# Four split-weight buffers given start addresses of their own in a three-pass float32 matmul kernel on one Trainium2 core

## The chip, the cores and the metric

The kernel runs on one core of a Trainium2 chip. The metric is the device time of one execution in microseconds (us). The profile calls the engines PE (TensorE, matmuls), PEld (TensorE's weight loads, which overlap its matmuls), DVE (VectorE), ACT (ScalarE), POOL (GpSimd) and SP (SyncE, which issues the loads). In a matmul one operand is stationary (the 128x128 block that a weight load brings into the array) and the other is moving (here mostly 128 partitions by 512 columns).

## The reference, cut to what matters

The reference is a stack of layers on 512 tokens of width 1024 in float32: a token mixer of four groups of heads, a short-convolution mixer, a latent attention, and three gated feed-forward layers of inner width 2816. Most of its arithmetic is products of activations with weight matrices:

```
x = x + mixed.astype(x.dtype) @ w_out[l]
x = x + conv_glu_ffn(rms_norm(x, norm2_g[l]), w_up[l], ffn_conv_w[l], ffn_conv_b[l], w_down[l])
...
u = h @ w_in
...
return (jax.nn.silu(g) * u) @ w2
```

## The kernel before, in words

**Weights.** The weight matrices are cut into 297 units of up to 1024 columns per partition (UNIT: eight 128x128 blocks, 4096 bytes in each partition). SP loads unit u into slot u % 4 of `raw` (L326, L338). ACT copies it into `whi` in the rounded type float32r (L352, slot u % 2), and DVE subtracts that from `raw` and writes the rest to `wlo` (L360, slot u % 2). So there are four split-weight buffers: two of `whi` and two of `wlo`.

**Products.** PE waits for the split of its unit and then does, for each 128-row block k, three matmuls (`passes`, L365 to L367): `whi` block times high part of the activation, `whi` block times low part, `wlo` block times high part. Each has its own weight load. The activations stand as `xhi`/`xlo`, `h_hi`/`h_lo`, `c_hi`/`c_lo`, `chi`/`clo` or `lhi`/`llo`, tiles of 512 columns. At the last matmul of a unit the semaphore `unit_used` goes up, which lets ACT split the unit after the next (L351). In one part of the latent attention `lhi`/`llo` are stationary and `whi`/`wlo` blocks are moving.

**Order.** The order of the work on every engine is written out by hand and synchronised by semaphores; nothing of it depends on an address. The matmuls that are not weight products (transposes, attention, scans) work on plain float32 tiles: `cst` (constant matrices), `mx`, `kn`, `qn`, `vtok` and others. Of them `pe_head_norm` (L876) has a block of `cst` stationary, and the attention logits (L1900, L1901) and outputs (L1610) have activations stationary.

**Addresses.** SBUF buffers are laid one after the other in the order of their declaration, each start rounded up to 32 bytes. Ahead of `whi` stand `xT`, `xhi`, `xlo` and `raw`, each 16384 bytes per partition, and the first of them starts 128 bytes past a multiple of 512. So do `xhi`, `xlo`, `raw`, both slots of `whi` and both of `wlo`. The buffers from `cst` up to the activations of the later layers take 27136 bytes (53 times 512), so that `h_hi`, `h_lo`, `c_hi`, `c_lo`, `lhi`, `llo`, `chi` and `clo` start at 128 past a multiple of 512 as well; `sq` starts at 416 past one. Each tile of 512 columns is 2048 bytes and each 128-column block 512 bytes. The blocks of `cst` used as stationary operands stand 516 bytes or 516 plus a multiple of 512 bytes into `cst`, that is at 132 past a multiple of 512.

Of the kernel before, what the change touches and what calls it, by code (L numbers as in the profile page):

```python
# [15 lines left out]
F32R = mybir.dt.float32r  # L16
I32 = mybir.dt.int32
ALU = mybir.AluOpType
ACT = mybir.ActivationFunctionType
AX = mybir.AxisListType  # L20

P = 128
# [13 lines left out]
UNIT = KT * P  # L36
RAW = 4
PARTS = 2
# [194 lines left out]
def build(nc, A, cst_d, out_d, known):  # L233
    ctx = ExitStack()
    with ctx:
        def sb(name, shape, dt=F32, c=ctx):
            return c.enter_context(nc.sbuf_tensor(name, shape, dt))

        def sem(name):
            return ctx.enter_context(nc.semaphore(name))  # L240
# [3 lines left out]
        xhi = sb("xhi", [P, KT, T], F32R)  # L244
        xlo = sb("xlo", [P, KT, T], F32R)
        raw = sb("raw", [P, RAW, UNIT])
        whi = sb("whi", [P, PARTS, UNIT], F32R)
        wlo = sb("wlo", [P, PARTS, UNIT], F32R)
        cst = sb("cst", [P, NCONST])
        pcol = sb("pcol", [P, NPCOL])  # L250
        gbias = sb("gbias", [P, 4])
# [29 lines left out]
        hi_split, lo_split, unit_used = sem("hi_split"), sem("lo_split"), sem("unit_used")  # L281
# [8 lines left out]
        v, a, g, t_ = nc.vector, nc.scalar, nc.gpsimd, nc.tensor  # L290

        def f32(ap):
            return ap.bitcast(F32)
# [13 lines left out]

        def unit_view(buf, u):
            _, kt, n, _ = UNITS[u]
            return buf[:, u % (RAW if buf is raw else PARTS), 0:kt * n].rearrange("p (k c) -> p k c", c=n)  # L310

        def is_past(u, i, per):
            return u + (per * i if isinstance(i, int) else 0) >= len(UNITS)

        def in_loop(value, i, per):
            return value if i is None else value + per * i

        def load_unit(sp, u):
            name, kt, n, pieces = UNITS[u]
            if u >= RAW:  # L320
                sp.wait_ge(lo_split, u - RAW + 1)
            at = 0
            for r0, c0, m in pieces:
                dst = unit_view(raw, u)[:, :, at:at + m]
                src = A[name][r0:r0 + kt * P, c0:c0 + m].rearrange("(k p) c -> p k c", p=P)
                sp.dma_start(dst, src).then_inc(unit_loaded[u % RAW], 16)  # L326
                at += m

        def load_loop(sp, stage, n_units, per, col):

            with sp.Fori(0, n_units // per) as i:
                for j in range(per):
                    u = FIRST[stage] + j
                    name, kt, n, pieces = UNITS[u]
                    r0 = pieces[0][0]
                    sp.wait_ge(lo_split, u - RAW + 1 + per * i)
                    src = A[name][r0:r0 + kt * P, bass.ds(col(i, j), n)].rearrange("(k p) c -> p k c", p=P)
                    sp.dma_start(unit_view(raw, u), src).then_inc(unit_loaded[u % RAW], 16)  # L338

        def elements(u, i, per):  # L340
            units = [UNITS[u]] + ([UNITS[u + per]] if i is not None and u + per < len(UNITS) else [])
            return max(kt * n for _, kt, n, _ in units)

        def split_hi(act, u, i=None, per=0):

            if is_past(u, i, per):
                return
            n = elements(u, i, per)
            act.wait_ge(unit_loaded[u % RAW], in_loop(LOADED[u], i, 16 * per // RAW))
            if u >= PARTS:  # L350
                act.wait_ge(unit_used, in_loop(u - PARTS + 1, i, per))  # L351
            a.activation(whi[:, u % PARTS, 0:n], raw[:, u % RAW, 0:n], ACT.Copy).then_inc(hi_split, 1)  # L352

        def split_lo(dve, u, i=None, per=0, e=v):

            if is_past(u, i, per):
                return
            n = elements(u, i, per)
            dve.wait_ge(hi_split, in_loop(u + 1, i, per))
            e.tensor_tensor(wlo[:, u % PARTS, 0:n], raw[:, u % RAW, 0:n], f32(whi[:, u % PARTS, 0:n]),  # L360
                            ALU.subtract).then_inc(lo_split, 1)

        def passes(out, wh, wl, xh, xl, first, last):
# [5 lines left out]
        def product(pe, u, tile, i=None, per=0, x=(xhi, xlo), k0=0, start=True, stop=True, ready=None, cols=0,  # L369
                    full=None, order=None, ks=None):  # L370


            kt = UNITS[u][1]
            pe.wait_ge(lo_split, in_loop(u + 1, i, per))
            for n, k in list(enumerate(order or range(kt)))[slice(*(ks or (0, kt)))]:
                if ready is not None:
                    ready(pe, k0 + k)
                wh, wl = (unit_view(b, u)[:, k, cols:cols + P] for b in (whi, wlo))
                last = passes(acc(tile), wh, wl, x[0][:, k0 + k, :], x[1][:, k0 + k, :],
                              start and n == 0, stop and n == kt - 1)  # L380
            if ks is None or ks[1] == kt:
                last.then_inc(*(step("pe", full) if full else (unit_used, 1)))
# [98 lines left out]
        def act_residual(act, stage, thirds, gain, following=None):  # L481
            per, np_, tiles = round_of(thirds)
            r0, n0 = NORM0[stage], TILE0[stage]

            def square(i, m):
                act.wait_ge(acc_free, n0 + m + 3 + tiles * i)
                act.wait_ge(summed, r0 + m + 1 + tiles * i)
                a.activation(sq[:, m % 2, :], tile_of(xT, m + tiles * i), ACT.Square).then_inc(squared, 1)  # L488

            def body(i, begun):  # L490
                for j in range(per):
                    m = j // np_
                    if begun and j == per - 1:
                        used = FIRST[stage] + KT // tiles * per
                        act_gain_all(act, begun, used, range(KT // 2))
                        square(i, m)
                        act_gain_all(act, begun, used, range(KT // 2, KT))
                    split_hi(act, FIRST[stage] + j + 2, i, per)
                    if j % np_ == np_ - 1 and not (begun and j == per - 1):
                        square(i, m)  # L500
                        if gain:
                            act.wait_ge(squared, r0 + m + 1 + tiles * i)
                            act_gained(act, gain, m + tiles * i)
            rounds(act, stage, KT // tiles, body, following)
# [53 lines left out]
        def act_up(act, stage, conv, h_hi, zS, yg, yu):  # L558
            u0, p0, n0 = FIRST[stage], PAIR0[stage], TILE0[stage]
            a.preload_act_table_set("silu_and_others")  # L560
            with act.Fori(0, FT // 2) as i:
                for j in range(4):
                    pair, is_up = j // 2, j % 2
                    m = pair + 2 * i
                    split_hi(act, u0 + j + 2, i, 4)
                    if conv:
                        mt = m + FT * is_up
                        act.wait_ge(prod_done, p0 + pair + 1 + 2 * i)
                        act.wait_ge(acc_free, n0 + j + 3 + 4 * i)
                        a.activation((yu if is_up else yg)[:, pair, :], zS[:, is_up, :], ACT.Identity,  # L570
                                     scale=ffn_w(2, mt), bias=ffn_b(mt)).then_inc(tap_done, 1)
                        if is_up:
                            act.wait_ge(conv_done, j + 2 + 4 * i)
                            a.activation(yg[:, pair, :], yg[:, pair, :], ACT.Silu).then_inc(gated, 1)
                    elif not is_up:
                        act.wait_ge(acc_free, n0 + j + 3 + 4 * i)
                        a.activation(yg[:, pair, :], zS[:, 0, :], ACT.Silu).then_inc(gated, 1)
                    if is_up:
                        act.wait_ge(prod_done, p0 + pair + 3 + 2 * i)
                        a.activation(tile_of(h_hi, m), xg[:, pair, :], ACT.Copy).then_inc(prod_hi, 1)  # L580
# [1833 lines left out]
def _program(nc, arrays, known):  # L2414

    aps = {n: nc.dram_tensor(f"in_{n}", a.shape, mybir.dt.from_np(a.dtype), kind="ExternalInput").ap()
           for n, a in arrays.items()}
    out = nc.dram_tensor("out_0", _OUT, F32, kind="ExternalOutput").ap()
    cst = aps.pop("constants")
    flat = {n: (x[0] if len(x.shape) == 3 and n in _WEIGHTS else x) for n, x in aps.items()}  # L2420
    return build(nc, flat, cst, out, known)
# [34 lines left out]
```

## Time and profile before

| | |
|---|---|
| time, 3 runs | 1982.45, 1982.6, 1985.07 us; median 1982.6 |
| profiled execution | 1982.77 us, span from first to last instruction 1981.0 us |
| mean granted TensorE clock | 0.985 of full speed |
| PE busy | 1905.2 us, 96% of the span |
| PEld busy | 1543.1 us, 78% |
| DVE, ACT, POOL busy | 997.3 us, 749.4 us, 228.9 us |

The profile is of one execution. A busy time counts from an instruction's start to its end, and matmuls overlap each other: one that takes 0.39 us can start 0.23 us after the one before. So the distance from start to start tells the pace of PE, not the duration of one.

### The profile page before, as it was taken

How to read it: one execution, taken by the hardware profiler on the slowest of the kernel's cores; microseconds unless marked ns; L12 is line 12 of the kernel's file. 1: busy time of each engine (PE TensorE's matmuls, PEld its weight loads, DVE VectorE, ACT ScalarE, POOL GpSimd, SP SyncE). 2: the span in 40 equal slices, each digit the busy share in tenths (PEclk: the TensorE clock that was granted, in tenths of full speed). 3: DMA queues.
4: the chain of work that ended last, by engine and by line, in shares of the span. 5: the costliest groups of instructions: out<-in, count | busy, mean ns of one | idle time of the engine just before them, and what ended most of it. 6: DMA issues, size and time to landing. Idle time of an engine off the chain costs nothing.

```text
span 1981.0 us, 25408 instructions
## 1 busy us (share of the span) xinstructions
PE 1905.2 (96%) x8897; PEld 1543.1 (78%) x8897; DVE 997.3 (50%) x1467; ACT 749.4 (38%) x1081; POOL 228.9 (12%) x196
## 2 busy tenths in 40 slices
PE   7989978889999999999999999999999999999998
PEld 6778856567788888888878888888776778888887
DVE  5463478754677774344454444433557443434322
ACT  5542543443544443232233323222455443222322
POOL 0051000012111111100021111110000111111100
PEclk9999989899999999999999999999999999999999
DMA  6310210011333333333333333333321123333332
GB/s 188 86 32 1 54 33 22 22 64 54 95 95 95 95 93 97 97 96 98 101 89 96 95 95 95 92 97 98 91 80 43 33 85 96 97 99 99 89 97 72
DMA packets 309219, 161.23 MB, mean 81 GB/s; under 512 B 12688, under 2 KB 306832, under 8 KB 309024
## 3 DMA queue, kind: packets, MB, share of 16 engines
q1 hardware_dynamic: 308080, 157.64, 27.6%
q0 software_dynamic: 640, 2.17, 0.3%
q8 instruction: 43, 0.70, 0.1%
q10 hardware_dynamic: 432, 0.52, 0.1%
q14 instruction: 24, 0.20, 0.0%
HBM read 158.21 MB, written 2.10 MB: 81 GB/s over the span
## 4 chain that ended last, share of the span: by engine, by line
PE 90%; DVE 5%; ACT 2%; issue 2%; DMA 1%; SPq 0%; POOL 0%; DVEq 0%; ACTq 0%; POOLq 0%
PE ps L365 26%; PE ps L367 26%; PE ps L366 26%; PE ps L1404 1%; PE ps L1019 1%; PE ps L1610 1%; PE ps L1419 1%; PE ps L1031 1%; PE ps L1900 1%; PE ps L1901 1%; PE ps L892 1%; PE ps L1395 1%; PE ps L1601 1%; DMA mx<-in_x 0%; PE ps L1239 0%
## 5 line engine op out<-in xcount | busy, mean ns | idle before, releaser
L365 PE MATMUL ps<-xhi,whi 128*128 128x512 f32 x1656 | 661.5, 399 | 10.1 <-DVE xlo L437 6.7
L366 PE MATMUL ps<-xlo,whi 128*128 128x512 f32 x1656 | 646.2, 390 | 0.0
L367 PE MATMUL ps<-xhi,wlo 128*128 128x512 f32 x1656 | 646.1, 390 | 0.0
L352 ACT ACTIVATE whi<-raw 128x1024 fp32r<-128x1024 f32 (+2 forms) x297 | 308.9, 1040 | 716.1 <-PE ps L367 713.5
L360 DVE TENSOR_TENSOR wlo<-raw,whi 128x1024 fp32r<-128x1024 f32 (+2 forms) x297 | 365.8, 1232 | 281.3 <-ACT whi L352 281.2
L365 PEld LDWEIGHTS ps<-xhi,whi 128*128 128x128 f32 x1656 | 312.0, 188 | 82.3 <-issue 5.4
L367 PEld LDWEIGHTS ps<-xhi,wlo 128*128 128x128 f32 x1656 | 311.8, 188 | 66.0
L366 PEld LDWEIGHTS ps<-xlo,whi 128*128 128x128 f32 x1656 | 312.1, 188 | 65.4 <-issue 3.7
L594 DVE TENSOR_TENSOR zS<-ps,rs 128x512 f32<-128x512 f32 x132 | 91.3, 692 | 293.7 <-PE ps L367 284.6
L367 PE MATMUL ps<-h_hi,wlo 128*128 128x512 f32 x528 | 205.4, 389 | 0.0
L365 PE MATMUL ps<-h_hi,whi 128*128 128x512 f32 x528 | 205.4, 389 | 0.0
L366 PE MATMUL ps<-h_lo,whi 128*128 128x512 f32 x528 | 205.4, 389 | 0.0
L619 POOL TENSOR_TENSOR h_lo<-xg,h_hi 128x512 f32 x66 | 84.9, 1286 | 646.3 <-ACT h_hi L580 646.3
L535 POOL TENSOR_TENSOR ssq<-ssq,sq 128x512 f32<-128x512 f32 x48 | 76.1, 1585 | 562.3 <-ACT sq L488 562.3
L366 PEld LDWEIGHTS ps<-h_lo,whi 128*128 128x128 f32 x528 | 99.1, 188 | 20.7
L367 PEld LDWEIGHTS ps<-h_hi,wlo 128*128 128x128 f32 x528 | 99.1, 188 | 20.7
L365 PEld LDWEIGHTS ps<-h_hi,whi 128*128 128x128 f32 x528 | 99.1, 188 | 20.2
L516 DVE TENSOR_TENSOR xT<-ps,xT 128x512 f32<-128x512 f32 (+1 forms) x48 | 33.2, 692 | 129.3 <-PE ps L367 129.3
L580 ACT ACTIVATE h_hi<-xg 128x512 f32 x66 | 41.7, 632 | 144.7 <-DVE xg L610 144.7
L1404 PE MATMUL ps<-mx,cst 128*128 128x512 f32 (+15 forms) x128 | 45.7, 463 | 27.1 <-DVE mx L1480 18.6
L1404 PEld LDWEIGHTS ps<-mx,cst 128*128 128x128 f32 x128 | 24.5, 212 | 41.5 <-DVE mx L1480 25.2
L437 DVE SCALAR_TENSOR_TENSOR xlo<-xT,pcol,xhi 128x512 fp32r<-128x512 f32 (+1 forms) x48 | 46.7, 1003 | 13.4 <-ACT xhi L431 13.2
(320 smaller groups left out, 1784.1 us busy)
## 6 DMA issues: line engine op xcount, KB each, us to landing
raw<-in_conv_ffn_w SPq DMA_DIRECT2D x52, 512.0 KB, 3.8
raw<-in_mla_ffn_w SPq DMA_DIRECT2D x52, 512.0 KB, 3.8
raw<-in_w_up SPq DMA_DIRECT2D x44, 512.0 KB, 3.7
raw<-in_w_in SPq DMA_DIRECT2D x28, 512.0 KB, 3.8
raw<-in_conv_w_in SPq DMA_DIRECT2D x24, 512.0 KB, 3.7
raw<-in_w_down SPq DMA_DIRECT2D x16, 448.0 KB, 3.6
raw<-in_conv_ffn_w SPq DMA_DIRECT2D x16, 448.0 KB, 3.6
raw<-in_mla_ffn_w SPq DMA_DIRECT2D x16, 448.0 KB, 3.6
```

Source lines behind the costliest of these rows:

```text
L352: a.activation(whi[:, u % PARTS, 0:n], raw[:, u % RAW, 0:n], ACT.Copy).then_inc(hi_split, 1)
L360: e.tensor_tensor(wlo[:, u % PARTS, 0:n], raw[:, u % RAW, 0:n], f32(whi[:, u % PARTS, 0:n]), ALU.subtract).then_inc(lo_split, 1)
L365: t_.matmul(out, wh, xh, start=first, stop=False)
L366: t_.matmul(out, wh, xl, start=False, stop=False)
L367: return t_.matmul(out, wl, xh, start=False, stop=last)
L437: v.scalar_tensor_tensor(tile_of(xlo, k), tile_of(xT, k), gain_of(name, k), f32(tile_of(xhi, k)), ALU.mult, ALU.subtract).then_inc(x_lo, 1)
L516: v.tensor_tensor(x, acc(m), x, ALU.add).then_inc(acc_free, 1)
L535: g.tensor_tensor(ssq[:, :], ssq[:, :], sq[:, m, :], ALU.add).then_inc(summed, 1)
L580: a.activation(tile_of(h_hi, m), xg[:, pair, :], ACT.Copy).then_inc(prod_hi, 1)
L594: v.tensor_tensor(z, acc(j), rs[:, :], ALU.mult).then_inc(acc_free, 1)
L619: g.tensor_tensor(tile_of(h_lo, m + 2 * i), xg[:, m, :], f32(tile_of(h_hi, m + 2 * i)), ALU.subtract).then_inc(prod_lo, 1)
L1404: t_.matmul(out[:, 0:n], C(red), PROD[j % 3][:, 0:n], start=True, stop=True).then_inc(*step("pe", f"{nm} intra{j} {vi} full"))
```

## The change

`whi` and `wlo` become four tensors, each of one unit (4096 bytes per partition), with unused gaps of 64, 64, 128 and 256 bytes behind them. Nothing but addresses is altered: the same instructions in the same order read and write buffers at 128 (`whi_a`), 192 (`whi_b`), 256 (`wlo_a`) and 384 (`wlo_b`) bytes past a multiple of 512. The gaps come to 512 bytes, so that every buffer behind them moves up by 512 bytes.

```
-        whi = sb("whi", [P, PARTS, UNIT], F32R)
-        wlo = sb("wlo", [P, PARTS, UNIT], F32R)
+        whi_a = sb("whi_a", [P, UNIT], F32R)
+        gap_a = sb("gap_a", [P, 16])
+        whi_b = sb("whi_b", [P, UNIT], F32R)
+        gap_b = sb("gap_b", [P, 16])
+        wlo_a = sb("wlo_a", [P, UNIT], F32R)
+        gap_c = sb("gap_c", [P, 32])
+        wlo_b = sb("wlo_b", [P, UNIT], F32R)
+        gap_d = sb("gap_d", [P, 64])
+        whi, wlo = (whi_a, whi_b), (wlo_a, wlo_b)
...
-            return buf[:, u % (RAW if buf is raw else PARTS), 0:kt * n].rearrange("p (k c) -> p k c", c=n)
+            slot = raw[:, u % RAW, 0:kt * n] if buf is raw else buf[u % PARTS][:, 0:kt * n]
+            return slot.rearrange("p (k c) -> p k c", c=n)
...
-            a.activation(whi[:, u % PARTS, 0:n], raw[:, u % RAW, 0:n], ACT.Copy).then_inc(hi_split, 1)
+            a.activation(whi[u % PARTS][:, 0:n], raw[:, u % RAW, 0:n], ACT.Copy).then_inc(hi_split, 1)
...
-            e.tensor_tensor(wlo[:, u % PARTS, 0:n], raw[:, u % RAW, 0:n], f32(whi[:, u % PARTS, 0:n]),
+            e.tensor_tensor(wlo[u % PARTS][:, 0:n], raw[:, u % RAW, 0:n], f32(whi[u % PARTS][:, 0:n]),
```

## Rows read from the trace of the kernel before

**Rows 1.** The page: busy time of each engine, and the chain that ended last.

```profile
span 1981.0 us, 25408 instructions
...
PE 1905.2 (96%) x8897; PEld 1543.1 (78%) x8897; DVE 997.3 (50%) x1467; ACT 749.4 (38%) x1081; POOL 228.9 (12%) x196
...
PE 90%; DVE 5%; ACT 2%; issue 2%; DMA 1%; SPq 0%; POOL 0%; DVEq 0%; ACTq 0%; POOLq 0%
PE ps L365 26%; PE ps L367 26%; PE ps L366 26%; PE ps L1404 1%; PE ps L1019 1%; PE ps L1610 1%; PE ps L1419 1%; PE ps L1031 1%; PE ps L1900 1%; PE ps L1901 1%; PE ps L892 1%; PE ps L1395 1%; PE ps L1601 1%; DMA mx<-in_x 0%; PE ps L1239 0%
```

**Rows 2.** Three stretches: length, busy time and count by engine, clock, DMA.

```profile
620.00:820.00 200.00, 200.00 (x884) 165.60 (x883) 115.95 (x130) 74.91 (x96) 23.14 (x18) 1.00 0.33 95
1120.00:1420.00 300.00, 300.00 (x1324) 248.12 (x1323) 115.13 (x122) 90.23 (x107) 34.22 (x27) 1.00 0.34 97
1720.00:1900.00 180.00, 180.00 (x796) 149.10 (x795) 66.71 (x74) 53.40 (x65) 21.91 (x17) 1.00 0.33 96
```

**Rows 3.** Timeline of PE in a feed-forward layer: start us, duration us, instruction.

```profile
1250.00 0.39 PE L365 MATMUL ps<-xhi,whi 128*128 128x512 f32 x1
...
1251.59 0.39 PE L366 MATMUL ps<-xlo,whi 128*128 128x512 f32 x1
```

**Rows 4.** Timeline of the weight loads in the same stretch.

```profile
1250.00 0.19 PEld L366 LDWEIGHTS ps<-xlo,whi 128*128 128x128 f32 x1
1250.23 0.19 PEld L367 LDWEIGHTS ps<-xhi,wlo 128*128 128x128 f32 x1
```

**Rows 5.** Groups by line and shape, PE: busy us, mean ns | idle before.

```profile
L365 PE MATMUL ps<-xhi,whi 128*128 128x512 f32 x1656 | 661.5, 399 | 10.1 <-DVE xlo L437 6.7 <-DVE wlo L360 3.4
...
L365 PE MATMUL ps<-h_hi,whi 128*128 128x512 f32 x528 | 205.4, 389 | 0.0
...
L365 PE MATMUL ps<-c_hi,whi 128*128 128x512 f32 x64 | 25.6, 399 | 2.2 <-POOL c_lo L619 2.2
...
L365 PE MATMUL ps<-chi,whi 128*128 128x512 f32 x36 | 14.9, 415 | 0.3 <-ACT qp L1949 0.3
...
L365 PE MATMUL ps<-lhi,whi 128*128 128x512 f32 x16 | 7.1, 444 | 0.0
...
L365 PE MATMUL ps<-whi,lhi 128*128 128x512 f32 x16 | 6.4, 402 | 1.4 <-ACT vtok L1936 1.4
```

**Rows 6.** Timeline of PE in the attention logits, plain float32.

```profile
1500.20 1.02 PE L1900 MATMUL ps<-kn,qn 128*128 128x512 f32 x2
1501.06 1.02 PE L1901 MATMUL ps<-kpz,qp 128*128 128x512 f32 x2
```

**Rows 7.** Timeline of PE where a block of cst is stationary.

```profile
94.39 1.88 PE L876 MATMUL ps<-sq,cst 128*128 128x512 f32 x4
```

**Rows 8.** Groups by line and shape, weight loads (PEld): busy us, mean ns.

```profile
L365 PEld LDWEIGHTS ps<-xhi,whi 128*128 128x128 f32 x1656 | 312.0, 188 | 82.3 <-issue 5.4 <-DVE xT L516 4.2 <-DVE xlo L437 2.9
...
L1019 PEld LDWEIGHTS ps<-mx 128*128 128x128 f32 x224 | 27.5, 205 | 0.9 <-POOL mx L981 0.9
...
L1901 PEld LDWEIGHTS ps<-kpz,qp 128*128 128x128 f32 x64 | 11.6, 190 | 6.4 <-issue 3.8
...
L1900 PEld LDWEIGHTS ps<-kn,qn 128*128 128x128 f32 x64 | 9.9, 190 | 0.7 <-ACT mla_P L1625 0.3
...
L876 PEld LDWEIGHTS ps<-sq,cst 128*128 128x128 f32 x32 | 6.2, 195 | 4.5 <-issue 3.1 <-ACT sq L858 0.5 <-DVE mx L883 0.2
...
L1826 PEld LDWEIGHTS ps<-qn,cst 128*128 128x128 f32 x10 | 1.9, 189 | 1.6 <-issue 1.4
```

**Rows 9.** Line views of both splits, 1250 to 1258: min/median/max ns, first to last start.

```profile
L352 ACT ACTIVATE whi<-raw x2: 1062/1062/1062, 1251.6 to 1257.0; 128x1024 fp32r<-128x1024 f32 x2
...
L360 DVE TENSOR_TENSOR wlo<-raw,whi x1: 1225/1225/1225, 1252.7 to 1252.7; 128x1024 fp32r<-128x1024 f32 x1
```

**Rows 10.** Tile wlo, whole span: all its splits, and its readiness as a cause of waiting.

```profile
L360 DVE TENSOR_TENSOR wlo<-raw,whi x297: 952/1226/1710, 14.4 to 1960.0; 128x1024 fp32r<-128x1024 f32 x127, 128x896 fp32r<-128x896 f32 x19, 128x768 fp32r<-128x768 f32 x3
```

## The prediction

> **What bounds the kernel now.** I read the page first: PE is busy for 96% of the span, and the chain that ended last lies on PE for 90% of it, 78% on the three lines of `passes` alone [rows 1]. A kernel in that state is as long as its matmuls are apart, so the next view is a table of stretches in the long feed-forward layers. There PE is busy for all of 200, 300 and 180 us, at a granted clock of 1.00, which is the 2.4 GHz level; it starts 884, 1324 and 796 matmuls in them [rows 2]. Divided, that is 226.2, 226.6 and 226.1 ns per matmul, a little low since a matmul cut by the edge of a stretch counts. The timeline gives the pace itself: from 1250.00 to 1251.59 us there are seven starts after the first, so 227 ns from each to the next [rows 3]. The three passes come at one pace, through layers in which DVE is busy for 58% of the time and for 37% of it [rows 2], so what sets the pace is in PE and its operands and not in what the other engines happen to do.
>
> The number to keep is what 227 ns is made of. 512 columns at 2.4 GHz are 213.3 ns; the pace is 13.3 ns more, or 544 clock periods where the tile has 512 columns. The next weight load starts with the running matmul (1250.00 and 1250.00 us) and lasts 188 ns, so it is over some 38 ns before the next start [rows 3, 4, 8]. Whether those 13.3 ns are a fixed price of changing weights, or two reads of SBUF in each other's way, is the whole question, because addresses are all that is changed.
>
> **The change part by part.** No instruction is added, removed or moved, and no wait. Four things get other addresses.
>
> *Weight loads from `whi_b`, `wlo_a` and `wlo_b`.* The lines of L365 add up to 1656 + 528 + 64 + 36 + 16 = 2300 blocks with weights stationary [rows 5], so 6900 loads for three passes. Two thirds come from `whi`, and units alternate between its slots: 2300 each from `whi_a` and `whi_b`, 1150 each from `wlo_a` and `wlo_b`. `whi_a` stays at 128, so 4600 loads read from a new phase. The trace has no float32r matmul at another phase: the moving tiles too start at 128 past a multiple of 512, all of them. The nearest rows are the plain float32 matmuls. L1900 and L1901 have both operands at multiples of 512 from 128, and L1901 starts 0.86 us after the first of two L1900, 430 ns each [rows 6]. L876 has a `cst` block at 132 stationary and `sq` at 416 moving; its four last 1.88 us in all, and with 0.59 for the last one (1.02 - 0.43 by the logits) the starts are 430 ns apart [rows 6, 7]. The loads themselves take 190 ns from `qn` and `qp` and 189 from `cst` at L1826; the 195 of L876 and 205 of L1019 are means over groups with some longer ones [rows 8]. So two pairs of phases, the stationary ones not even 16-byte aligned to each other, give one pace and nearly one load. That is the value I take: 4600 times 0 = 0. It doesn't prove it for float32r, where the moving tile goes by at twice the pace and has half as much room for a second reader. The bound below is that all 13.3 ns go: 4600 x 13.3 = 61 us gained. The bound above is the longest of these load rows, if the 38 ns between a load's end and the next start stay as they are: 205 + 38 = 243 ns, 16 more than now, 4600 x 16 = 74 us lost.
>
> The Trainium skill speaks on this (SBUF — State Buffer, "Who interferes with whom"): PE has one read port for the moving operand and an independent one for weight loads, and never waits on another engine. By it the loads' phase costs and gains nothing, and the sum is the same 0; but it leaves the 13.3 ns unexplained, and no row here shows the ports.
>
> *The v part of the latent attention*, with `whi`/`wlo` blocks moving and `lhi`/`llo` stationary: 16 blocks of three passes [rows 5], 48 matmuls. At the same bounds, 48 x 13.3 = 0.6 us either way, two thirds of them moved; 0 taken.
>
> *The splits.* ACT writes `whi` in 1062 ns and DVE reads it and writes `wlo` in 1225 ns. What hides them is the unit in the array: ACT starts at 1251.6 us, DVE ends at 1252.7 + 1.2 = 1253.9, and the release of the next slot, with which PE goes on to this unit, is at 1257.0, 3.1 us later [rows 9]. A split would have to grow by more than its own length to be seen. Where there is less cover, in the mixers and at the layers' starts, PE waited for `wlo` for 3.4 us of the whole span [rows 5]; splits slower by a tenth would make that less than 1 us more. The spread that is already there, 952 to 1710 ns [rows 10], includes smaller units and meetings with POOL, and the latter don't depend on 64 bytes. 0 taken.
>
> *Everything behind*, from `cst` on, moves by 512 bytes and keeps its phase, so the loads, stores and 1949 other matmuls (8897 less 6900 and 48) see no other alignment. 0.
>
> The sum: 0 + 0 + 0 + 0. The profiled execution took 1982.77 us, 0.2 us from the median 1982.6 of the runs, so I predict the median, 1982.6 us. Within 0.2% of it, 1978.6 to 1986.6, is about what a measurement of this kernel can't tell from no change; the three runs alone spread over 2.6 us.
>
> **Rival 1: faster, the reads were in each other's way.** For it: the excess is 32 periods per 512 columns and keeps to the same value in every layer, which reads in step with each other would give, and a weight block and its moving tile stand at one phase in every float32r pair. Plain float32 matmuls, at half the pace, have almost no excess: 430 ns for what would be 426.7 [rows 6]. Against it: the load ends well before the matmul does, so a shift of 64 bytes shifts the meeting in time more than it undoes it; and a fixed price would look the same. If the excess fell to the 3.3 ns of the float32 rows in the moved loads, 4600 x 10 = 46 us go and the time is 1937 us; with all of it gone, 1922. If only the `wlo` loads (2300) gain, 1960. The sign to look for is a pace that differs between buffers, L365 to L367 in units of odd number against even ones.
>
> The Trainium skill has a rule of this kind (TensorE: Matmul & The Clock Gate, "Back-to-back issue gap"): at full clock one matmul follows another by N/2.4 + 2.5 ns, 216 for 512 columns. The trace doesn't agree, at 227 ns; if the alignment were why, the rule would make it 4600 x 11 = 51 us less, an estimate of 1932 us.
>
> **Rival 2: slower, one phase was what kept them apart.** The mechanism: with moving tile and weight block at one phase, the two reads go through SBUF in step; at 64, 128 and 256 bytes' distance some meet, and a load or a matmul grows. It costs where the array is never idle, so each nanosecond counts: 0.2% of 1982.6 is 4.0 us, over 4600 loads 0.86 ns each, and that is the point from which it decides. At the upper bound, 16 ns, the time is 1982.6 + 74 = 2056 us; should just the 2300 `wlo` loads take the mean load of L876, 7 ns more, it is 1982.6 + 16 = 1999 us. Against it stand the 430 ns at both pairs of phases [rows 6, 7].
>
> **Rival 3: a small drift,** 4 to 10 us either way, from a few waits and clock drops that fall otherwise, in the mixers, where the chain leaves PE for 10% of the span [rows 1]. Nothing is changed there in kind, and the three runs say 2.6 us.
>
> **How the numbers follow.** No change 0.82; rival 1, 0.08; rival 2, 0.07; rival 3, 0.03, shared between the signs. That gives faster by over 0.2% 0.09, within 0.2% 0.83, slower 0.08. The range is that of the likeliest case, which alone holds 8 in 10: 1978.6 below and, as one of the runs stood 2.5 us above the median, a little over 1986.6 above, so 1978 to 1988. The unknown costs' bounds, 1922 and 2056, belong to the rivals and are left outside; they hold less than 2 in 10 together.
>
> **What would show it.** In the profile of the changed kernel: 25408 instructions [rows 1]; the three stretches with 884, 1324 and 796 matmuls within one or two; loads of 188 ns from all four buffers; both splits at about 1062 and 1225 ns; PE at 96%. The prediction is wrong if the starts of L365 to L367 are apart by anything but 227 ns in any buffer: 217 says rival 1, over 228 rival 2. If they stand at 227 and the time is still off, the step on the splits or the other buffers has failed, and waits for `wlo` at L365 would show above 3.4 us.

## The result, and the profile after

The changed kernel takes 2015.92 us (median of 4 runs, 2012.94 to 2017.64) against 1982.96 us (4 runs, 1982.45 to 1985.07): a ratio of 1.0161, 95% interval 1.0148 to 1.0173, or 33 us more. It is slower, and the time lies outside the range of the prediction.

The page of the changed kernel, its head and its chain, beside [rows 1]:

```profile
span 2014.3 us, 25408 instructions
...
PE 1938.3 (96%) x8897; PEld 1548.3 (77%) x8897; DVE 994.3 (49%) x1467; ACT 751.4 (37%) x1081; POOL 229.5 (11%) x196
...
PE 90%; DVE 5%; ACT 2%; issue 2%; SPq 0%; DMA 0%; POOL 0%; DVEq 0%; ACTq 0%; POOLq 0%
```

The instructions are the same, and so is the chain, to a point in the shares. PE's busy time is up by 33.1 us, which is the whole loss; PEld's is up by 5.2 us, 0.6 ns per load, and DVE, ACT and POOL are within 3 us. Nothing waits for anything new. Three stretches of the feed-forward layers show it, beside [rows 2] (length, busy time and count of PE, PEld, DVE, ACT, POOL, then the granted clock):

```profile
620.00:820.00 200.00, 200.00 (x866) 162.77 (x865) 116.71 (x135) 76.20 (x96) 21.76 (x18) 1.00 0.32 94
1140.00:1440.00 300.00, 300.00 (x1297) 243.83 (x1296) 112.58 (x120) 88.35 (x107) 34.31 (x27) 1.00 0.33 94
1750.00:1930.00 180.00, 180.00 (x780) 146.49 (x779) 65.54 (x72) 51.99 (x64) 21.97 (x17) 1.00 0.33 95
```

At the same clock, 2.4 GHz, PE starts 866 matmuls in the first stretch where it started 884: 200/866 = 230.9 ns against 226.2. The rows by line tell the buffers apart. These are the down projections, whose moving tiles are `h_hi` and `h_lo` (busy us, mean ns of one | idle before); a unit in slot a is read from `whi_a` and `wlo_a`, one in slot b from `whi_b` and `wlo_b`:

```profile
L374 PE MATMUL ps<-h_lo,whi_b 128*128 128x512 f32 x264 | 104.8, 397 | 0.0
L375 PE MATMUL ps<-h_hi,wlo_a 128*128 128x512 f32 x264 | 104.6, 396 | 0.0
L374 PE MATMUL ps<-h_lo,whi_a 128*128 128x512 f32 x264 | 104.5, 396 | 0.0
L375 PE MATMUL ps<-h_hi,wlo_b 128*128 128x512 f32 x264 | 104.0, 394 | 0.0
L373 PE MATMUL ps<-h_hi,whi_a 128*128 128x512 f32 x264 | 103.2, 391 | 0.0
L373 PE MATMUL ps<-h_hi,whi_b 128*128 128x512 f32 x264 | 102.7, 389 | 0.0
```

Before, each of the three passes was 389 ns, the first in [rows 5] and the other two in the same view:

```profile
L366 PE MATMUL ps<-h_lo,whi 128*128 128x512 f32 x528 | 205.4, 389 | 0.0
L367 PE MATMUL ps<-h_hi,wlo 128*128 128x512 f32 x528 | 205.4, 389 | 0.0
```

There a matmul was 389 ns and its successor started 227 ns after it, so about 162 ns of a duration overlap the next one and the rest is the pace; what a duration has above 389 is taken as time lost. The six rows come to 623.8 us for 1584 matmuls, 393.8 ns each, 4.8 ns more than before; times the 6948 float32r matmuls that is 33 us. (In what follows "excess" is this number for a slot: its three h rows, divided by 792, less 389.0. The ends of matmuls are modelled in the profile, so behind it, in brackets, stands the same from the start times in the trace: the mean from one start to the next, less the 226.7 ns of the kernel before. The two differ by up to 1.1 ns.) Slot a, in which `whi_a` has not moved in phase, has 5.3 ns (4.9) and slot b 4.3 (4.6). The 4968 matmuls with x tiles went the same way, from a mean of 393.3 ns to 398.5.

The loads have hardly changed, beside the 188 ns of [rows 8], and neither have the splits, in the view by line and shape over all engines:

```profile
L368 DVE TENSOR_TENSOR wlo_a<-raw,whi_a 128x1024 fp32r<-128x1024 f32 x127 | 156.3, 1231 | 97.0 <-ACT whi_a L360 97.0
...
L360 ACT ACTIVATE whi_a<-raw 128x1024 fp32r<-128x1024 f32 x127 | 134.6, 1059 | 399.8 <-PE ps L375 398.6 <-DMA raw<-in_w_in 1.2
...
L375 PEld LDWEIGHTS ps<-h_hi,wlo_b 128*128 128x128 f32 x264 | 49.6, 188 | 10.2
L374 PEld LDWEIGHTS ps<-h_lo,whi_a 128*128 128x128 f32 x264 | 49.6, 188 | 11.3
...
L1908 PE MATMUL ps<-kn,qn 128*128 128x512 f32 x16 | 8.2, 593 | 0.0
```

The last row is the attention logit matmul in plain float32, and it has not moved either. Before:

```profile
L1900 PE MATMUL ps<-kn,qn 128*128 128x512 f32 x16 | 8.2, 593 | 0.0
```

### The profile page after: what moved, and what is told of

Read it like the earlier page. It is cut to its first block, busy times and chain, and to the rows that moved or that the text cites. A ratio compares the mean times of both kernels' runs of the same rounds, so it can differ in the third digit from the quotient of the medians.

```text
span 2014.3 us, 25408 instructions
## 1 busy us (share of the span) xinstructions
PE 1938.3 (96%) x8897; PEld 1548.3 (77%) x8897; DVE 994.3 (49%) x1467; ACT 751.4 (37%) x1081; POOL 229.5 (11%) x196
## 4 chain that ended last, share of the span: by engine, by line
PE 90%; DVE 5%; ACT 2%; issue 2%; SPq 0%; DMA 0%; POOL 0%; DVEq 0%; ACTq 0%; POOLq 0%
PE ps L374 26%; PE ps L375 26%; PE ps L373 26%; PE ps L1412 1%; PE ps L1027 1%; PE ps L1618 1%; PE ps L1427 1%; PE ps L1039 1%; PE ps L1908 1%; PE ps L1909 1%; PE ps L900 1%; PE ps L1609 1%; PE ps L1403 1%; SPq L334 0%; PE ps L1711 0%
## 5 line engine op out<-in xcount | busy, mean ns | idle before, releaser
L373 PE MATMUL ps<-xhi,whi_b 128*128 128x512 f32 x824 | 330.5, 401 | 7.8 <-DVE xlo L445 4.6
L373 PE MATMUL ps<-xhi,whi_a 128*128 128x512 f32 x832 | 333.8, 401 | 2.0 <-DVE xlo L445 2.0
L375 PE MATMUL ps<-xhi,wlo_a 128*128 128x512 f32 x832 | 330.6, 397 | 0.0
L374 PE MATMUL ps<-xlo,whi_a 128*128 128x512 f32 x832 | 330.6, 397 | 0.0
L374 PE MATMUL ps<-xlo,whi_b 128*128 128x512 f32 x824 | 328.2, 398 | 0.0
L375 PE MATMUL ps<-xhi,wlo_b 128*128 128x512 f32 x824 | 326.0, 396 | 0.0
L368 DVE TENSOR_TENSOR wlo_a<-raw,whi_a 128x1024 fp32r<-128x1024 f32 (+2 forms) x149 | 180.0, 1208 | 149.1 <-ACT whi_a L360 149.1
L368 DVE TENSOR_TENSOR wlo_b<-raw,whi_b 128x1024 fp32r<-128x1024 f32 (+2 forms) x148 | 182.9, 1236 | 139.8 <-ACT whi_b L360 139.7
L373 PEld LDWEIGHTS ps<-xhi,whi_b 128*128 128x128 f32 x824 | 155.9, 189 | 51.9 <-DVE xT L524 4.2
L373 PEld LDWEIGHTS ps<-xhi,whi_a 128*128 128x128 f32 x832 | 159.5, 192 | 40.0 <-DVE kraw L2026 2.1
L374 PEld LDWEIGHTS ps<-xlo,whi_a 128*128 128x128 f32 x832 | 157.4, 189 | 35.6 <-issue 1.4
L375 PEld LDWEIGHTS ps<-xhi,wlo_a 128*128 128x128 f32 x832 | 157.2, 189 | 34.5
L375 PEld LDWEIGHTS ps<-xhi,wlo_b 128*128 128x128 f32 x824 | 155.7, 189 | 32.6
L375 PE MATMUL ps<-h_hi,wlo_a 128*128 128x512 f32 x264 | 104.6, 396 | 0.0
```

Source lines behind the costliest of these rows:

```text
L368: e.tensor_tensor(wlo[u % PARTS][:, 0:n], raw[:, u % RAW, 0:n], f32(whi[u % PARTS][:, 0:n]), ALU.subtract).then_inc(lo_split, 1)
L373: t_.matmul(out, wh, xh, start=first, stop=False)
L374: t_.matmul(out, wh, xl, start=False, stop=False)
L375: return t_.matmul(out, wl, xh, start=False, stop=last)
```

## The experiments

**Theories.** M: the pace depends on how far, in bytes, the weight block starts from the moving tile (below: the distance, 0 before the change, and 0, 64, 128 and 256 for `whi_a`, `whi_b`, `wlo_a`, `wlo_b` after it). S: it depends on the step in phase from one weight block to the next. A: some starts are bad in themselves. Each kernel below computes the same as the kernel before; only the lines that declare the buffers differ from the changed kernel, whose own four gaps are taken out in all of them. The rows shown of each are those by line and shape: busy us, mean ns of one | idle before; the three lines of `passes` lie between L370 and L375 there, always in the order `whi` with the high part, `whi` with the low part, `wlo`. While a matmul runs, the block of the next one is loaded, so an interval from start to start has one block in use and another on its way. "whi, wlo" of a slot means both of its buffers, and each kernel but e4 ends its gaps so that everything behind keeps its phase.

### e1: all four at distance 64

```
+        gap0 = sb("gap0", [P, 16])
         whi_a = sb("whi_a", [P, UNIT], F32R)
         whi_b = sb("whi_b", [P, UNIT], F32R)
         wlo_a = sb("wlo_a", [P, UNIT], F32R)
         wlo_b = sb("wlo_b", [P, UNIT], F32R)
+        gap1 = sb("gap1", [P, 112])
```

> All four buffers at 192 past a multiple of 512, the moving tiles still at 128. Theory M (the pace depends on how far the weight block stands from the moving tile): the distance is 64 in every load, so the pace leaves 227 ns, to 229 to 236, and the time is 1998 to 2030 us. Theory S (it depends on the step in phase from one weight block to the next): every step is 0 as before the change, the pace is 227 ns and the time 1983 us. Theory A (192, 256 or 384 are bad starts in themselves): 192 is one of them, slower as by M.

Measured: 2027.07 us, ratio 1.0218 (1.0189 to 1.0248). Slower than the change itself, with no step anywhere, so S falls as the whole cause. One row of slot a and one of slot b:

```profile
L371 PE MATMUL ps<-h_hi,whi_b 128*128 128x512 f32 x264 | 104.3, 395 | 0.0
...
L373 PE MATMUL ps<-h_hi,wlo_a 128*128 128x512 f32 x264 | 104.3, 395 | 0.0
```

All six are at 395: an excess of 6.1 ns (6.7), and 6948 x 6.1 = 42 us, of the 43 measured.

### e2: slot a at 0, slot b at 64

```
         whi_a = sb("whi_a", [P, UNIT], F32R)
         wlo_a = sb("wlo_a", [P, UNIT], F32R)
+        gap0 = sb("gap0", [P, 16])
         whi_b = sb("whi_b", [P, UNIT], F32R)
         wlo_b = sb("wlo_b", [P, UNIT], F32R)
+        gap1 = sb("gap1", [P, 112])
```

> Slots a (whi and wlo) at 128, slots b at 192. Within a unit all loads have one phase; only units differ. M and A: units in slots a keep 227 ns, units in slots b go to 229 to 236, time 1983 plus half of some 32, about 1990 to 2005 us. S: only the one load per unit that changes slot steps, 297 loads of at most 9 ns, so 1983 to 1986 us, both slots at 227 ns inside a unit.

Measured: 2009.78 us, ratio 1.0131 (1.0102 to 1.0161), some 5 us above the range that M gave: half of e1's 43 us would be 2006, and slot a was not quite free.

```profile
L371 PE MATMUL ps<-h_hi,whi_b 128*128 128x512 f32 x264 | 104.5, 396 | 0.0
L373 PE MATMUL ps<-h_hi,wlo_b 128*128 128x512 f32 x264 | 104.4, 396 | 0.0
L372 PE MATMUL ps<-h_lo,whi_b 128*128 128x512 f32 x264 | 104.4, 395 | 0.0
L372 PE MATMUL ps<-h_lo,whi_a 128*128 128x512 f32 x264 | 103.0, 390 | 0.0
L373 PE MATMUL ps<-h_hi,wlo_a 128*128 128x512 f32 x264 | 102.9, 390 | 0.0
L371 PE MATMUL ps<-h_hi,whi_a 128*128 128x512 f32 x264 | 102.7, 389 | 0.0
```

The slots go their own ways, unit by unit, in one run: 6.6 ns (6.7) in slot b, 0.6 (0.8) in slot a. So one run can measure two distances, to about 1 ns. The writes by ACT and DVE are not what is met. They go into the slot that PE is not reading, and in e1 the start times give 233.3 ns from start to start both in the intervals in which a split is running and in those in which none is.

### e3: whi at 0, wlo at 128

```
         whi_a = sb("whi_a", [P, UNIT], F32R)
         whi_b = sb("whi_b", [P, UNIT], F32R)
+        gap0 = sb("gap0", [P, 32])
         wlo_a = sb("wlo_a", [P, UNIT], F32R)
         wlo_b = sb("wlo_b", [P, UNIT], F32R)
+        gap1 = sb("gap1", [P, 96])
```

> Both whi at 128, both wlo at 256. S: two of three loads step by 128 or minus 128; they go to some 233 ns as in slot a of the changed kernel, the third stays at 227 to 229; 1982.6 + 6900 x 4.8 ns = about 2014 us. M and A: only the wlo loads are away from 128, one load in three is slower, by up to 9 ns: 2300 x 9 = 20 us, about 1990 to 2004 us, and the two intervals in which whi is loaded stay at 227.

Measured: 2010.68 us, ratio 1.0136 (1.0106 to 1.0165): above M's range and nearer to the number of S.

```profile
L373 PE MATMUL ps<-h_hi,wlo_a 128*128 128x512 f32 x264 | 104.8, 397 | 0.0
...
L372 PE MATMUL ps<-h_lo,whi_a 128*128 128x512 f32 x264 | 104.5, 396 | 0.0
...
L371 PE MATMUL ps<-h_hi,whi_a 128*128 128x512 f32 x264 | 102.7, 389 | 0.0
```

During L372 the next block, from `wlo`, is loaded: 7 ns longer, as M has it. During L373 a `whi` block at distance 0 is loaded, and that is 8 ns longer too, which M in its simple form did not give and S did. S as the whole cause fell with e1; what is left of it is that an interval's cost is not only that of the load in it.

### e4: all operands moved by 64, distances kept

```
+        front = sb("front", [P, 16])
         xT = sb("xT", [P, KT, T])
```

> 64 bytes ahead of the first buffer, so that all operands, moving and stationary, stand at 192 and keep their distances. M and S: 227 ns and 1983 us. A: every load is from a bad start, the pace is above 229 ns and the time above 1998 us.

Measured: 1983.73 us (8 runs), ratio 1.0001 (0.9990 to 1.0012). All h rows are back at 389 ns, as this one is:

```profile
L370 PE MATMUL ps<-h_hi,whi_a 128*128 128x512 f32 x264 | 102.7, 389 | 0.0
```

A falls for 192, which is as good a start as 128 if the moving tile is there too. It is also the control for taking the tensors apart, which costs nothing.

### f1 to f4, g2, g4, h2: other distances, two per run

These test three theories, named in the texts below: R, that the cost repeats at a shorter step of the distance than 512 bytes; L, that every distance but 0 costs alike; G, that some distance is better than 0. All runs have the shape of e2; slot a and slot b stand at the two distances in the name. Distances of 4, 16, 208 and 240 are not multiples of 32 and are made by a slice of a larger buffer. As examples:

```
+        gap0 = sb("gap0", [P, 32])                                  # f2
         whi_a = sb("whi_a", [P, UNIT], F32R)
         wlo_a = sb("wlo_a", [P, UNIT], F32R)
+        gap1 = sb("gap1", [P, 32])
...
-        whi_b = sb("whi_b", [P, UNIT], F32R)                        # g4
+        whi_b = sb("whi_b", [P, UNIT + 8], F32R)[:, 1:1 + UNIT]
```

> whi and wlo of slot a 32 bytes from the moving tile's phase, of slot b 96 bytes. Theory L (only distance 0 is good, any other costs about what 64 did, 6.6 ns a matmul): both slots at some 233 ns, time about 2027 us. Theory R (SBUF repeats at a shorter step than 512, so that some distances are as good as 0): 32 and 96 are not whole multiples of 64, so they go to 233 ns too unless the step is 32. Theory G (some distance is better than 0, down to 216 ns): one of the two slots below 227 ns.

> Slot a at distance 128, slot b at distance 256. L: both at 233 ns, about 2027 us. R: with a step of 128 both are back at 227 ns and the time at 1984 us; with a step of 256 only slot b, about 2005 us. G: a slot below 227 ns.

> Slot a at distance 384 (minus 128), slot b at 448 (minus 64). L: both at 233 ns, about 2027 us. R: as the same steps say, slot a back at 227 ns with a step of 128, else 233; slot b 233. G: if the sign of the distance matters, one of these is below 227 ns where 64 and 128 are above.

> Slot a at distance 16, slot b at distance 192. L: both at 233 ns, about 2027 us. If the cost grows with the distance, slot a stays near 227 ns and slot b at 233, about 2005 us. G: one below 227 ns.

> Slot a at distance 224, slot b at 240, that is 32 and 16 short of 256. Theory R with a cost that depends on the distance on the far side: 192 and 448 took 229 ns, so 224 and 240 take 227 to 230 ns and the time is 1984 to 2005 us. Theory L (any distance that isn't a multiple of 256 costs about 6 ns): both at 233 ns, about 2027 us. Theory G: one of them below 227 ns and the time below 1980 us.

> Slot a at distance 320, slot b at distance 4. R: slot a as at 64, some 233 ns. Slot b: if a 16-byte piece of SBUF is the unit in which reads meet, 4 bytes is partly in the same piece and takes 227 to 231 ns; if it is only a matter of the phase in time, 4 bytes are one column or 0.4 ns and it keeps 227. Time 1983.5 + 3450 x 6.6 ns = about 2006 us with slot b at 227, and up to 2018 us with it at 231.

> Slot a at distance 160, slot b at 208. From the distances so far (128 to 232.6 ns, 192 to 229.1, 224 to 233.2, 240 to 227.4) both lie between 227 and 234 ns and the time between 1990 and 2027 us. Theory G, some distance is better than 0: a slot below 226.6 ns.

Measured (ratio with its 95% interval; excess of a slot from its three h rows, in brackets from the start times):

| run | time us | ratio | slot a: distance, excess | slot b: distance, excess |
|---|---|---|---|---|
| f1 | 2028.48 | 1.0225 (1.0195 to 1.0255) | 32, 6.6 ns (6.7) | 96, 7.2 ns (7.3) |
| f2 | 2004.91 | 1.0106 (1.0077 to 1.0136) | 128, 5.6 ns (5.7) | 256, 0.5 ns (0.5) |
| f3 | 2010.17 | 1.0133 (1.0103 to 1.0162) | 384, 5.6 ns (5.9) | 448, 2.7 ns (2.5) |
| f4 | 2006.84 | 1.0116 (1.0087 to 1.0145) | 16, 2.0 ns (2.1) | 192, 2.5 ns (2.4) |
| g2 | 2010.30 | 1.0131 (1.0111 to 1.0152) | 224, 6.1 ns (6.8) | 240, 1.8 ns (1.9) |
| g4 | 2021.86 | 1.0190 (1.0169 to 1.0210) | 320, 5.4 ns (6.5) | 4, 4.9 ns (5.7) |
| h2 | 2023.35 | 1.0199 (1.0169 to 1.0229) | 160, 6.3 ns (7.0) | 208, 4.7 ns (5.2) |

Rows by line and shape of f2, where slot a (128) stands at 395 ns and slot b (256) is back at 389:

```profile
L372 PE MATMUL ps<-h_hi,whi_a 128*128 128x512 f32 x264 | 104.3, 395 | 0.0
...
L372 PE MATMUL ps<-h_hi,whi_b 128*128 128x512 f32 x264 | 102.7, 389 | 0.0
```

And of slot b of g4, where 4 bytes cost 5 ns:

```profile
L372 PE MATMUL ps<-h_lo,whi_b 128*128 128x512 f32 x264 | 104.0, 394 | 0.0
```

Distances that differ by 256 agree, by the start times: 0 and 256 (0.8, 0.5), 128 and 384 (5.7, 5.9), 192 and 448 (2.4, 2.5), 64 and 320 (6.7, 6.5). So theory R holds with a repeat of 256 bytes where both buffers of a slot share one distance, and L, all distances alike, falls: 192 and 240 cost about a third of 64 or 96. G falls as far as it was looked for: at fifteen distances other than 0 no slot's mean is below 389 ns, or below 226.7 from start to start. Not all came out as expected: g2 took 2010 us against 2005 at most and g4 2022 against 2018; 448 cost 2.5 ns where 6 were expected, the cost of 64; and f4 met its 2005 us with 2 ns in each slot and not 6 in one.

One distance does not have one cost. In f4 slot a has 2.0 ns with the h tiles, while with the x tiles its three rows are at 405, 395 and 394 against a mean of 393 before, 4.5 ns. By the start times, slot a of f4 has two paces, unit by unit. In all three down projections its first four units with h tiles are at 233.2 to 233.4 ns and the eight after them at 226.6 to 226.7, the pace of distance 0. After the first of the three it stays there through the x units that follow, up to 1004 us, where the x units before it, read from the same buffers, were at 233.3 to 233.4; at 1059 us, after some 50 us of other work, it is back at 233.3. One unit at each pace, from 766.7 and from 797.3 us:

```profile
L371 PE MATMUL ps<-h_hi,whi_a 128*128 128x512 f32 x8 | 3.2, 394 | 0.0
L371 PE MATMUL ps<-h_hi,whi_a 128*128 128x512 f32 x8 | 3.1, 389 | 0.0
```

So the 2.0 ns of 16 bytes is 12 units with the full cost and 24 with none. The same addresses can give either.

### g1: the weights left alone, the moving tiles moved

```
+        front = sb("front", [P, 48])
         xT = sb("xT", [P, KT, T])
...
+        gap0 = sb("gap0", [P, 80])
         whi_a = sb("whi_a", [P, UNIT], F32R)
...
+        gap1 = sb("gap1", [P, 16], c=mla)
         qn = sb("qn", [P, NH2, T], c=mla)
+        gap2 = sb("gap2", [P, 112], c=mla)
```

> All weight buffers back at 128; xT, xhi, xlo and raw at 320 instead, h_hi and h_lo at 128 as before. If the distance between the two operands is what counts, with a repeat of 256 bytes (theory R), the x passes are at distance 320, which is 64 past a multiple of 256, and take 233 ns, the h passes 227 ns: 4968 x 6.6 ns = 33 us, about 2016 us. If something about the weight buffers themselves counts, everything is at 227 ns and 1984 us. Besides, qn (stationary) stands 64 bytes from kn (moving) in the attention logits, plain float32: if the slower stream hides the meeting, L1900 keeps its 430 ns from start to start; if not, it goes up by 6 ns or more.

`front` pushes `xT`, `xhi`, `xlo` and `raw` to 320, and `gap0` puts the weights back to 128.

Measured: 2014.26 us, ratio 1.0151 (1.0131 to 1.0172).

```profile
L372 PE MATMUL ps<-xlo,whi_a 128*128 128x512 f32 x832 | 329.9, 396 | 0.0
L373 PE MATMUL ps<-xhi,wlo_a 128*128 128x512 f32 x832 | 329.7, 396 | 0.0
...
L371 PE MATMUL ps<-h_hi,whi_b 128*128 128x512 f32 x264 | 102.7, 389 | 0.0
L373 PE MATMUL ps<-h_hi,wlo_b 128*128 128x512 f32 x264 | 102.7, 389 | 0.0
...
L1908 PE MATMUL ps<-kn,qn 128*128 128x512 f32 x16 | 8.2, 593 | 0.0
```

This is the run that settles what counts. From the same weight buffers, the x passes lose 6 ns and the h passes nothing, according to where the other operand stands. And the logits, whose operands are now 64 bytes apart, stay at 593 ns: plain float32 does not show the effect.

### g3: the change in whole steps of 256 bytes

```
-        gap_a = sb("gap_a", [P, 16])
+        gap0 = sb("gap0", [P, 64])
```

and so behind each of the four: `whi_a` and `wlo_a` at 128, `whi_b` and `wlo_b` at 384.

> The change made again with whole steps of 256 bytes: whi_a and wlo_a at 128, whi_b and wlo_b at 384, a gap of 256 bytes behind each. R: all at 227 ns, 1984 us, the same as before. If different starts of the buffers cost something in themselves, above 1990 us.

Measured: 1984.14 us (10 runs) against 1984.16 us (13 runs), ratio 1.0003 (0.9994 to 1.0013).

```profile
L375 PE MATMUL ps<-h_hi,wlo_a 128*128 128x512 f32 x264 | 102.7, 389 | 0.0
L373 PE MATMUL ps<-h_hi,whi_b 128*128 128x512 f32 x264 | 102.7, 389 | 0.0
```

Four buffers apart, two phases, and no loss.

### h1: whi_b alone at 64

```
         wlo_b = sb("wlo_b", [P, UNIT], F32R)
+        gap0 = sb("gap0", [P, 16])
         whi_b = sb("whi_b", [P, UNIT], F32R)
+        gap1 = sb("gap1", [P, 112])
```

> Only whi_b is moved, to 192; the other three buffers at 128. If 256 is as good as 0, slot b behaves as in the changed kernel: intervals of some 226, 236 and 232 ns, 231.4 in the mean, slot a at 227: 1983.5 + 3450 x 4.7 ns = about 2000 us. If wlo_b at 384 had a share in the changed kernel, slot b is faster than 231.4 ns. If each load had a price of its own by its distance, the intervals in which whi_b is loaded would take 233 ns and the one in which wlo_b is loaded 227; if the cost is carried over from one matmul to the next, the one with the unmoved wlo_b is not 227.

Measured: 2008.89 us, ratio 1.0126 (1.0097 to 1.0156); 2000 was expected.

```profile
L371 PE MATMUL ps<-h_hi,whi_b 128*128 128x512 f32 x264 | 105.1, 398 | 0.0
L373 PE MATMUL ps<-h_hi,wlo_b 128*128 128x512 f32 x264 | 104.8, 397 | 0.0
L372 PE MATMUL ps<-h_lo,whi_b 128*128 128x512 f32 x264 | 103.5, 392 | 0.0
```

A miss. Slot b has an excess of 6.7 ns here (and slot a, unmoved, 1.0) and 4.3 in the changed kernel, where `wlo_b` stands 256 further. So the times of single loads cannot be added up, and 256 and 0 did not come to the same here: in this run the two intervals with a `whi_b` load are 9 and 8 ns longer and the one with `wlo_b` 3, in the changed kernel it is 0 and 5 for the first two and 8 for the last. In both runs part of the cost falls in an interval whose own load is at distance 0 or 256. Since f4 shows two paces at the same addresses, it is not shown that the 256 bytes make the difference: it may be the way into the pattern.

The start times show how long a cost is carried. They were averaged over the 12 stretches of exactly 24 h matmuls from one slot (in ns from start to start; the other slot was read just before each stretch; the last interval, in which the other slot's block is loaded, is left out):

| run, slot | first intervals | then |
|---|---|---|
| e2, slot a (0; before it 64) | 228.2, 232.6, 230.8 | 226.6 to 226.8 |
| h1, slot a (0; before it 64 and 0) | 230.8, 236.0, 228.2, 232.5, 230.7 | 226.3 to 226.8 |
| changed kernel, slot a (0 and 128; before it 64 and 256) | 232.4, 235.0, 230.9, 230.9, 230.8, 232.4, 230.9, 232.4 | 234.2, 226.6, 232.6, over and over |
| e3, slot a (0 and 128; before it the same) | 226.5, 232.5, 234.2 | the same, over and over |

The excess of a slot at distance 0 thus lies in the first intervals behind a unit at another distance, three to six of them over all h stretches, and the changed kernel's slot a reaches the pattern of e3 after eight. It is hardly the split that starts at the same moment: in h1, slot a with x tiles, the first five intervals are 231.9, 233.2, 227.9, 232.8 and 230.6 ns where no split was running (4 to 16 cases each) and 231.0, 235.4, 228.3, 232.5 and 230.6 where one was, and in g3 and e4 the same splits run and the first intervals stay at 226 to 227.

No distance tried beats the kernel before, so there is no version to offer that is faster than both.

## Why the prediction was wrong, point by point

**What bounds the kernel** was right, and is why the change shows at all: PE is hardly ever idle, so 4.8 ns per matmul become 33 us.

**The step that failed** is the first term, the weight loads from the moved buffers: "4600 times 0 = 0". It measured 33 us, 7.2 ns per moved load. The zero was carried over from plain float32 rows, L876, L1900 and L1901, to float32r pairs, of which the trace of before has none at another distance. The text itself said that this does not prove it for float32r, whose moving tile goes by at twice the pace, and took the zero all the same. g1 shows the gap directly: at 64 bytes float32 keeps its 593 ns and float32r loses 6 ns, in one run. The agreement of the two float32 pairs was thus no evidence for the case asked, and should not have carried 0.82.

**Rival 2** is what happened: slower, decided at 0.86 ns per load, with 1999 us for the `wlo` loads at 7 ns and 2056 us as the bound. The measured 2016 lies between. Its mechanism was half right. The distance to the moving tile does it (e1, e4, g1), but not through a longer load: with h tiles the loads stay at 188 to 190 ns (192 in the longest x group of the changed kernel), and what grows is the time from the end of a load to the next start, in e1 from 36 ns to 43. The upper bound of the prediction had let the load grow and held this time fixed. The split into buffers was wrong as well: e3 and h1 show that the cost doesn't stay with the moved load, so slot a loses 5.3 ns with one of its two buffers unmoved.

**Rival 1** did not come. The 13.3 ns above 213.3 at distance 0 remain at their value; no distance gave any of them back. Whether they are a fixed price is not shown, only that fifteen distances did not touch them.

**The splits and everything behind** were right. In their longest form the splits took 1059 (slot a) and 1060 ns (slot b) on ACT and 1231 and 1269 on DVE, and PE's wait for `wlo` is 3.3 us, against 3.4:

```profile
L373 PE MATMUL ps<-xhi,whi_b 128*128 128x512 f32 x824 | 330.5, 401 | 7.8 <-DVE xlo L445 4.6 <-DVE wlo_b L368 3.3
```

e4 moves all of them and g3 everything behind, at no cost. **The v part** shared the wrong zero, at a size that doesn't count: there the `whi`/`wlo` blocks are the moving side, and the matmuls went from 402, 391 and 389 ns to between 392 and 409, some 5 ns each, 48 x 5 = 0.2 us.

**The rules that the prediction cited.** The Trainium skill (SBUF — State Buffer, "Who interferes with whom") gives PE two independent read ports and lets it wait on no one. That rule would have made the distance free. The measurement decides: it is worth 0 to 7 ns per matmul in float32r. That two reads of SBUF meet is still only argued; what the runs show is that the pace depends on the two operands' addresses relative to each other. The other rule, weighed at rival 1 (the Trainium skill, TensorE: Matmul & The Clock Gate, "Back-to-back issue gap"), is given there for an isolated matmul, and the prediction took it for a stream of loads and matmuls. No run here reaches its 216 ns: the shortest time from start to start of a float32r pair in any of the sixteen traces is 224.

**Open**: why the cost repeats at 256 bytes, by what it is carried into intervals with a load at distance 0, what decides between the two paces at 16 bytes, and why a slot with mixed distances does not follow the table. No run took the weight load away from under the matmul, so that the two reads meet was not tested by itself.

## What to carry to other kernels

In a kernel bound by back-to-back float32r matmuls with a weight load each, keep the stationary blocks and the moving tiles at the same address modulo 256 bytes; a small buffer or a pad between them can cost 1 to 2% without any wait showing in the profile. If such a kernel slows after a change that only moved buffers, look at the mean duration of the matmuls by operand name, not at the waits. And a zero that is read from rows of another data type is a guess, to be priced as one.

## What the runs showed of the hardware that was not expected

A distance of 4 bytes between weight block and moving tile costs 4.9 ns of some 227 per matmul (g4), 96 bytes 7.2 ns (f1), 256 bytes nothing (g3). Plain float32 matmuls of the same shape do not notice 64 bytes (593 ns in both). The pace depends on history: behind a unit at 64 bytes, matmuls at distance 0 need three to six intervals to come back to 226.7 ns (e2, h1), and at 16 bytes the same slot runs at 233.4 ns for a stretch of units and at 226.6 for another (f4).
